# A mixer and mixture-of-experts kernel: a ninth weight slot, a bias write on another queue, and a rebuilt router chain

## The reference

```python
# first block: two layers of three kinds of attention behind one input projection
h = _layernorm(x, ln_in_g, ln_in_b)
for layer in range(2):
    proj = einsum('bsd,de->bse', h, w_in[layer])
    ya, yb, yc = differential(proj), forgetting(proj), stick_breaking(proj)
    y = concat([ya, yb, yc]) @ w_out[layer]
    h = _layernorm(alpha * h + y, ln_g[layer], ln_b[layer])

# second block: sparse attention and a state-space mixer, then 32 experts, 4 per token
mod = silu(c) @ w_ada + b_ada                    # sh_m, sc_m, g_m, sh_f, sc_f, g_f
h = _rms(x, norm_mix) * (1 + sc_m) + sh_m
mixed = sigmoid(g_attn) * y_attn + sigmoid(g_ssd) * y_ssd
x = x + g_m * (mixed @ w_out)
h = _rms(x, norm_ffn) * (1 + sc_f) + sh_f
x = x + g_f * _moe(h, ...)

# _moe
logits = h @ w_router + b_router                 # 256 x 32
top_val, top_idx = top_k(logits, 4)
gates = softmax(top_val)
# each expert, on its tokens: gu = xb @ w_gu[e] + b_gu[e]; clipped SwiGLU;
# out = act @ w_dn[e] + b_dn[e], weighted with the gate and summed per token
```

## Time and profile before

| what | value |
|---|---|
| median of three runs | 1664.46 us (1664.18 to 1669.3) |
| profiled execution | 1668.54 us, span 1666.7 us |
| PE busy | 1564.5 us (94% of the span) |
| DVE, ACT, POOL busy | 417.0, 280.5, 20.1 us |
| chain that ended last | PE 74%, DMA 18%, DVE 4%, ACT 2% |
| mean rate of the DMA engines | 309 GB/s |
| bytes read from HBM | 511.21 MB |

### The profile page before, as it was taken

One profiled execution on the slowest core, in us unless ns is written; L12 is line 12 of the kernel. 1 busy time (PEld: TensorE's weight loads), 2 busy tenths in 40 slices (PEclk: granted clock), 3 DMA queues, 4 the chain that ended last, 5 costly groups with the idle time before them and its releaser, 6 DMA issues.

```text
span 1666.7 us, 18564 instructions
## 1 busy us (share of the span) xinstructions
PE 1564.5 (94%) x7605; PEld 878.2 (53%) x7605; DVE 417.0 (25%) x926; ACT 280.5 (17%) x555; POOL 20.1 (1%) x41
## 2 busy tenths in 40 slices
PE   7989999997999999989999999999999999998997
PEld 6757878685887778853333333333332333333232
DVE  2432113512345381232111211121211112111111
ACT  1224113323232332121000000000000000000000
POOL 4000000000000000000000000000000000000000
PEclk9989999998999999999999999999999999999999
DMA  9765563547232423639999999999999999999996
GB/s 258 194 199 193 185 220 103 200 174 269 101 126 85 152 101 132 266 140 430 423 427 427 427 427 428 428 428 428 427 427 428 428 428 428 427 428 428 427 427 290
DMA packets 83775, 515.17 MB, mean 309 GB/s; under 512 B 4892, under 2 KB 8252, under 8 KB 59144
## 3 DMA queue, kind: packets, MB, share of 16 engines
q1 hardware_dynamic: 82488, 513.45, 76.5%
q0 software_dynamic: 1200, 0.92, 0.7%
q10 hardware_dynamic: 32, 0.01, 0.0%
HBM read 511.21 MB, written 3.15 MB: 309 GB/s over the span
## 4 chain that ended last, share of the span: by engine, by line
PE 74%; DMA 18%; DVE 4%; ACT 2%; issue 1%; SPq 0%; ACTq 0%; DVEq 0%
PE psum L482 25%; PE psum L1109 19%; PE psum L1197 10%; DMA w_down<-in_w_gu 8%; DMA ring<-in_w_gu 8%; PE psum L1083 4%; PE psum L491 3%; DMA ring<-in_w_in 3%; PE psum L1092 2%; PE psum L1100 1%; PE psum L541 1%; PE psum L522 1%; PE psum L627 1%; PE psum L1185 1%; DVE hidden L2137 1%
## 5 line engine op out<-in xcount | busy, mean ns | idle before, releaser
L482 PE MATMUL psum<-spare,ring 128*128 128x256 f32 x1504 | 335.7, 383 | 4.8 <-ACT spare L1421 4.3
L482 PEld LDWEIGHTS psum<-spare,ring 128*128 128x128 f32 x1504 | 285.6, 191 | 54.7 <-issue 15.4
L1109 PE MATMUL psum<-ring,hg 128*64 128x512 f32 x1024 | 229.4, 596 | 8.1 <-DMA ring<-in_w_gu 8.0
L1109 PE MATMUL psum<-w_down,hg 128*64 128x512 f32 x768 | 172.5, 596 | 8.9 <-DMA w_down<-in_w_gu 8.9
L1109 PEld LDWEIGHTS psum<-ring,hg 128*64 128x64 f32 x1024 | 69.8, 137 | 152.0 <-issue 135.2
L1197 PE MATMUL psum<-ring,hiddenT 128*64 128x512 f32 x512 | 113.4, 595 | 13.9 <-ACT hiddenT L1648 10.9
L1109 PEld LDWEIGHTS psum<-w_down,hg 128*64 128x64 f32 x768 | 52.3, 137 | 120.9 <-issue 104.1
L2128 DVE TENSOR_SCALAR gu<-psum 128x512 f32<-128x512 f32 x32 | 22.1, 692 | 329.8 <-PE psum L1109 329.8
L2140 DVE TENSOR_TENSOR o_slot<-psum,gain_rows 128x512 f32<-128x512 f32 x32 | 22.1, 692 | 320.5 <-PE psum L1197 320.5
L1197 PE MATMUL psum<-w_down,hiddenT 128*64 128x512 f32 x384 | 85.9, 595 | 12.9 <-issue 7.7
L1197 PEld LDWEIGHTS psum<-ring,hiddenT 128*64 128x64 f32 x512 | 38.0, 137 | 79.0 <-issue 79.0
(11 more groups left out here) (406 smaller groups left out, 1318.9 us busy)
## 6 DMA issues: line engine op xcount, KB each, us to landing
ring<-in_w_gu SPq DMA_DIRECT2D x64, 2048.0 KB, 27.6
w_down<-in_w_gu SPq DMA_DIRECT2D x48, 2048.0 KB, 28.2
ring<-in_w_dn SPq DMA_DIRECT2D x32, 2048.0 KB, 31.8
ring<-in_w_in SPq DMA_DIRECT2D x24, 2048.0 KB, 9.1
w_down<-in_w_dn SPq DMA_DIRECT2D x24, 2048.0 KB, 31.0
spare<-in_w_gu SPq DMA_DIRECT2D x16, 2048.0 KB, 29.0
ring<-in_w_ada SPq DMA_DIRECT2D x12, 2048.0 KB, 9.2
spare<-in_w_dn SPq DMA_DIRECT2D x8, 2048.0 KB, 33.1
```

Of the source, the lines that this page charges most:

```text
L482: mm = pe.matmul(bank[0:m, c * T:(c + 1) * T], w[:, k, c0 + c * P:c0 + c * P + m], src[:, k, :], start=(i == 0), stop=(i == k_n - 1))
L1109: mm = pe.matmul(psum[half * CAP:(half + 1) * CAP, loop_bank(4 + part), :], hg[:, k, side, :], w[:, c0:c0 + 512], start=False, stop=(k == ...
```

## The change

- **A ninth slot.** `xT`, `condT`, `mod_rows`, `stat`, `biasrev` and `w_router` become parts of one tile `nine` of 16 KB per partition, in the same total size. The experts use it as ninth slot once `xT` has been read for the last time (`residual` at 4). `SLOTS` is 9, an expert's loads go round nine slots, two experts are written out ahead of a loop over six, and SP's conditions follow. The load into `spare` waits for the router's products instead of the last copy of `h_tok`.
- **The bias write** is issued by POOL, after `w_router`'s load, instead of by SP after `ada0`.
- **Norms.** The last norm of the first block squares each pair of chunks on ACT one pair behind its normalisation; "m." then neither loads the table nor squares. Of the eight sums of squares of "f.", four stand ahead of the last output product.
- **Router.** Three residual groups stand ahead of the router, the transposes of all chunks come first, then the eight router products one after the other in the eighth bank; the fourth residual group follows when DVE has read the logits. The choice is made by `max` over 32 logits, a copy of the four largest, `match_replace` of these by -3e38, and one comparison, for both token blocks. Positions and `pick` are made at once, the gates after them; the turned gates come inside the first expert, ahead of its third put. Of the rows of positions, three and the memset come after the gates.

```diff
@@ the slots
-    FOURS = NE // 4
-    SLOTS = 8
+    SIXES = (NE - 2) // 6
+    SLOTS = 9
@@ PE
             for i in range(2):
                 features(f"wo{2 * j + i}", w, zg, 256 * i, 2)
+                if j and not i:
+                    square_sums_of("f.", range(0, 4))
             last_of(f"wo{j}", f"wo{2 * j + 1}")
-        norm_sums("f.", None)
-        take("router4")
+        square_sums_of("f.", range(4, KC))
+        def residual(k):
+            b, j = k // 2, k % 2
+            for i in range(4):
+                mm = pe.matmul(psum[:, loop_bank(k), i * P:(i + 1) * P], xT[:, 4 * j + i, b * P:(b + 1) * P],
+                               ident[:, :], start=(i == 0), stop=False, skip_group_check=True)
+            mm.then_inc(ev("residual"), 1)
+        for k in range(3):
+            take(f"sum{k}")
+            residual(k)
...
-            mm = pe.matmul(psum[q, banks["router4"][0], 0:T], w_router[:, c, :], hT[:, c, :],
-                           start=(c < 4), stop=(c >= 4), skip_group_check=True)
...
+        for c in range(KC):
+            q = slice(32 * (c % 4), 32 * (c % 4) + 32)
+            mm = pe.matmul(psum[q, BANKS, 0:T], w_router[:, c, :], hT[:, c, :], start=(c < 4), stop=(c >= 4),
+                           skip_group_check=True)
+        mm.then_inc(ev("router4"), 1)
...
+        pe.wait_ge(ev("logits_read"), 1)
+        residual(3)
...
-        pe.wait_ge(ev("chosen"), 1)
+        pe.wait_ge(ev("selected"), 1)
         bank = take("pos")
...
+        def turn_gates():
+            for b in range(NB):
+                for half in range(2):
+                    pe.matmul(psum[half * HEAD:half * HEAD + NE, loop_bank(7), T + b * P:T + (b + 1) * P],
+                              rt[:, 1, b, :], ident[:, :], start=True, stop=True)
@@ SP
-            if name == "ada0":
-                read_out(sp, "bias")
-                sp.dma_start(bias_dram[:, :, :], biasrev[:, :].rearrange("h (o j) -> h o j", o=1)
-                             .broadcast_to([AH, P, 2 * T])).then_inc(ev("bias_out"), 16)
...
-            if j < 2:
-                sp.wait_ge(ev(f"down_done{j}"), n - 1)
-            elif j < 5:
-                sp.wait_ge(ev("gu_used"), 3 * n + j - 4)
+            if j == 0:
+                sp.wait_ge(ev("gu_done"), 2 * n - 2)
+            elif j < 3:
+                sp.wait_ge(ev(f"down_done{j - 1}"), n - 1)
             else:
-                sp.wait_ge(ev("gu_done"), 2 * n)
+                sp.wait_ge(ev("gu_used"), 3 * n + j - 5)
...
-        read_out(sp, "ht11")
+        sp.wait_ge(ev("router4"), 1)
         load(0, 1, 1, 1)
-        for j in range(2, 6):
+        sp.wait_ge(ev("residual"), 4)
+        load(0, 1, 1, 2)
+        for j in range(3, 6):
             load_after(0, 1, 1, j)
@@ POOL, after the load of w_router
+        read_out(pool, "bias")
+        pool.dma_start(bias_dram[:, :, :], biasrev[:, :].rearrange("h (o j) -> h o j", o=1)
+                       .broadcast_to([AH, P, 2 * T])).then_inc(ev("bias_out"), 16)
@@ ACT, in norm
+                if then_square and j:
+                    square(n, j - 1)
+            if then_square:
+                square(n, 3)
@@ DVE
         for b in range(NB):
-            top_sum(rt[:, 2, b, :], rt[:, 0, b, :], rt[:, 3, b, :], rt[:, 4, b, :],
-                    rsm[:, 8 * b + TOPE - 1:8 * b + TOPE], rsm[:, 16 + b:17 + b], rsm[:, 18 + b:19 + b], TOPE)
+            ch.after(dve.match_replace(rt[:, 3, b, :], four[:, b, :], rt[:, 2, b, :], -3e38))
+        tt(rt[:, 0, :, :], rt[:, 3, :, :], rt[:, 2, :, :], ALU.is_lt, ev("selected"))
```

More of the change, by code:

```diff
@@ L282, in mixer_moe_kernel @@
     rsm = sb("rsm", [P, 32], where=third)
+    four = sb("four", [P, NB, 8], where=third)
     pos = sb("pos", [P, NB, 5, NE], where=third)
@@ L536, in norm_sums, with square_sums_of @@
                 ada(aside)
-            bank = take(tag + "var")
-            for c in range(KC):
+            square_sums_of(tag, range(KC))
+        def square_sums_of(tag, cs):
+            if cs[0] == 0:
+                take(tag + "var")
+            bank = psum[:, banks[tag + "var"][0], :]
+            for c in cs:
                 if c % 2 == 0:
@@ L1065, in _ @@
         full(mm, "count")
-        bank = take("gateT")
-        for b in range(NB):
-            for half in range(2):
-                mm = pe.matmul(bank[half * HEAD:half * HEAD + NE, b * P:(b + 1) * P], rt[:, 1, b, :], ident[:, :],
-                               start=True, stop=True)
-        full(mm, "gateT")
         M = MAX_EXTRA
@@ L1402, in exp_table, with norm @@
             act.preload_act_table_set("natural_log_exp_and_others")
-        def norm(tag, centred, scale, shift, dst, e):
-            exp_table()
+        def norm(tag, centred, scale, shift, dst, e, squared=False, then_square=False):
             n = norms[0]
             norms[0] += 1
-            for j in range(4):
+            if not squared:
+                exp_table()
+            for j in range(0 if squared else 4):
                 r = slice(2 * j, 2 * j + 2)
@@ L1624, in _ @@
         ins.then_inc(ev("gate_exp"), 1)
-        rows_of_tokens(0, 1)
-        rows_of_tokens(1, 1)
-        for half in range(2):
-            r = slice(half * HEAD, half * HEAD + NE)
-            read("gateT", gateT[r, :], cols=slice(0, T), rows=r, last=half == 1)
         def gathered(n, width=2, first_bank=4):
@@ L1651, in _ @@
         gathered(1, first_bank=6)
+        act.wait_ge(ev("turned"), 1)
+        for half in range(2):
+            r = slice(half * HEAD, half * HEAD + NE)
+            act.activation(gateT[r, :], psum[r, loop_bank(7), T:2 * T], ACT.Copy).then_inc(ev("gateT"), 1)
         expert(0, 0)
@@ L2051, in _ @@
         both = lambda v: v.rearrange("p (b e) -> p b e", b=NB)
-        ch.after(dve.tensor_copy(quarters[:, :], product(dve, "router4")[:, 0:T]), ev("router_parts"))
+        ch.after(dve.memset(four[:, :, :], 3e38))
+        dve.wait_ge(ev("router4"), 1)
+        ch.after(dve.tensor_copy(quarters[:, :], psum[:, BANKS, 0:T]), ev("router_parts"))
         dve.wait_ge(ev("logits"), 1)
-        ch.free(dve.tensor_tensor(rt[:, 2, :, :], both(product(dve, "router4")[:, T:T + NB * NE]),
-                                  over(b_router[:, :], NB), ALU.add), "router4")
+        tt(rt[:, 2, :, :], both(psum[:, BANKS, T:T + NB * NE]), over(b_router[:, :], NB), ALU.add, ev("logits_read"))
@@ L2071, in _ @@
+        tt(rt[:, 0, :, :], rt[:, 3, :, :], rt[:, 2, :, :], ALU.is_lt, ev("selected"))
         ch.free(dve.scalar_tensor_tensor(rt[:, 3, :, :], both(product(dve, "pos")[:, 0:NB * NE]), 1.0, rt[:, 0, :, :],
                                          ALU.add, ALU.mult), "pos")
[L2073 to L2075 removed]
+        ts(pos[:, :, 0, :], rt[:, 3, :, :], -1.0, None, ALU.add)
@@ L2102, in _ @@
         ins.then_inc(ev("picked"), 1)
+        dve.wait_ge(ev("gate_exp"), 1)
+        for b in range(NB):
+            stt(rt[:, 5, b, :], rt[:, 5, b, :], 1.0, rt[:, 0, b, :], ALU.mult, ALU.mult,
+                accum_out=rsm[:, 22 + b:23 + b])
+        ch.after(dve.reciprocal(rsm[:, 24:26], rsm[:, 22:24]))
+        for b in range(NB):
+            ts(rt[:, 1, b, :], rt[:, 5, b, :], rsm[:, 24 + b:25 + b], None, ALU.mult)
         for side in (0, 1):
@@ L2106, in _ @@
         ins.then_inc(ev("gates"), 1)
+        for r in range(1, 4):
+            ts(pos[:, :, r, :], rt[:, 3, :, :], -1.0 - CAP * r, None, ALU.add)
+        ch.after(dve.memset(pos[:, :, 4, :], -1.0))
         ts(passes[:, 1:2], passes[:, 0:1], CAP + 0.5, None, ALU.is_gt)
```

107 lines of the change are left out of this document (45 added, 62 removed).

## The result

The changed kernel takes **1650.06 us** (median of four runs, 1648.38 to 1653.79) against 1664.61 us (1664.18 to 1669.3) for the kernel before on the same chip: ratio 0.991, 95% interval 0.989 to 0.9933. That is 14.6 us faster; 12.3 had been forecast, to 1652. The profiled execution of it took 1648.38 us, its span is 1646.5.

The account below looks back on a forecast made before the run. The end was set by when the weight stream restarts for good plus the loads left; slot -4.9, router chain -6.7, norm -2.7 and bias write +2 sum to -12.3 us, giving 1652, range 1638 to 1661.

Parts of the forecast that it names:

- Ninth slot, -4.9: Expert weight stream: the ninth slot's load is hidden before the restart, leaving 183 loads instead of 184, -4.9 us.
- Rival E: Expert stage: the slot does nothing, as PE sets the pace or the ninth load is late; 1657 us, chance 0.08.
- Sums of squares, +1.1: Norm ahead of the router: four of eight sums moved before the last output product make PE end later, +1.1 us.
- Residual groups in the wait for h, 0: Ahead of the router: three residual groups, 2.9 us, just fit PE's wait for the normalised h, cost 0.
- Router products in strips, with the copy at -2.7: Router: eight products overlap in four 32-column strips, 1.00 us, so the `quarters` copy starts 2.7 us earlier, the +1.1 included.
- VectorE's choice, -3.4: Router's choice of experts: fewer operations, and gates moved behind the picks, cut 5.4 us to 2.0, -3.4 us.
- Three position ops and a memset ... -0.6: Path to the first gather: these ops leave it, -0.9, the experts' bias product ends slightly after the picks, +0.3; -0.6 us.
- Norm of the first block, -2.7: Mixer's first block, last norm: earlier squares and no table load end the sums near 407.0 instead of 409.76, -2.7 us.
- Between 0 (order harmless) and +4.2 I take +2: Bias write moved to POOL's queue: packet-for-packet sharing delays loads in the kernel's start, 0 to +4.2, taken as +2 us.
- rival B: Kernel's start: the bias write gets out of the loads' way, -10 instead of +2, 1640 us, chance 0.20.
- Rival D: Kernel's start: POOL's write goes first on its 8 engines by long packets, +21.3, 1671 us, chance 0.07.
- Rival C: Router chain gives half: strips not overlapping, low clock in the transposes, norm at 0; 1658 us, chance 0.15.

Follow-up runs that it names:

- the second trace: The changed kernel run and profiled once more with nothing edited: 1650.39 us, ratio 0.9909 against the kernel before.
- `b_gu` first: Against the changed kernel, SP issues the load into `spare` only after POOL's four small gate/up bias loads have landed: 1647.86 us, ratio 0.9898.
- three at once: Changed kernel plus bias write from 128 partitions, eight sums of squares together, and `spare` load held until the gate/up bias lands: 1640.73 us, ratio 0.9857.

## Why the prediction was right, step by step

The sign held, and so did the argument on what bounds the kernel: the restart of the stream and the loads behind it. 1650.06 lies in the range and 2 us from the figure, but that it is so near is in part luck. The router chain gave 2.2 to 2.7 us less than forecast, the bias write 5 to 7 us more and by another mechanism than the one forecast, the norm 1.1 us more.

- **What bounds the kernel: right.** The end follows the restart: 15.42 us of the profile's 20.2 came by an earlier restart, 4.84 by one load less.
- **Ninth slot, -4.9: right.** 4.84 in the trace; 4.7 in the trace and 4.25 by medians when undone. Rival E is out.
- **Sums of squares, +1.1: right.** 1.22 measured up to the copy. PE idled 0.96 us ahead of the last of them.
- **Residual groups in the wait for h, 0: right.** Three groups take 2.84 us, and the transposes wait for ACT (0.70, 0.26 and 0.33 us), not ACT for PE.
- **Router products in strips, with the copy at -2.7: right.** 1.07 us for the eight, and the stretch to the copy is 42.97 - 40.60 = 2.4 shorter, the +1.2 in it. The 3.4 us of products that do not overlap did not come. To the restart the placement alone is worth 0.7 to 1.2 us, since without it there is no wait for `b_gu`.
- **VectorE's choice, -3.4: right.** 5.38 became 1.99. A `MATCH_REPLACE8` on 32 elements takes 0.18 us, its value load 0.09; I had bounded the two together by 0.28. The old choice puts the restart only 0.8 to 1.2 us later, for the same reason.
- **"Three position ops and a memset ... -0.6": the step that failed in the chain.** From the copy to the gather I had 5.9 to 6.0 us and measured 7.38 and 7.69. I gave the bias product 0.3 us behind the picks. It waited 0.74 us for `b_gu` (1.41 in the second trace), because the load into `spare`, which the change issues earlier, shares the engines with it; and then it ran 2.08 us at the low clock, where it takes 1.13 at the high. The prediction had hidden two loads "inside the time in which the stream stands still" and asked what they would do to PE's end, not what they would do to a small load that was due in that time. The window from 716 to 726 us shows the new traffic (columns as in the earlier trace rows; in the same ten microseconds counted from the copy, 729.25 to 739.25, the kernel before moved 210 GB/s):

```profile
716.00:726.00 10.00, 8.72 (x48) 6.91 (x48) 5.64 (x33) 1.90 (x4) 0.00 (x0) 0.66 0.96 398
```

  The low clock holds into the gather, 5.28 us instead of 4.84. So the chain from the output products to the restart gained 61.43 - 56.90 = 4.5 us (4.0 in the second trace), not 6.7. With `b_gu` first it gains 61.43 - 55.08 = 6.35 us, nearly the forecast, and 7.4 with the sums together as well (three at once).
- **Norm of the first block, -2.7: right, mis-sized.** 3.8 measured, within the ends of 0 and -4.6. After the table load is gone, the eight sums take 5.25 us in the chain and not 6.16, as only part of them meets the low clock.
- **"Between 0 (order harmless) and +4.2 I take +2": the term that failed.** It was -3 to -5: -3 to -4 by the traces (second value products at 111.0 in the mean instead of 114.1 and 115.3), -4.8 by the median. Both premises of the +2 were half right, and the prediction took the wrong side between them. Packets do go one for one, as I had worked out. But I summed up the engines' time as if the write would give some of it to the loads. It kept its 49 GB/s and the loads' 24 GB/s came on top, as fits a pace set at the source partitions and not by the order on the engines; that it is set there, the write from all partitions shows. It is rival B's mechanism, with about half its price or less: not all of a wait of 6.75 us and the clock behind it is gone, since one load packet per write packet is a slow pace too, and the next two loads were late by 0.92 and 3.37 us. B's full 10 us come when the write itself is fast: by medians 4.8 from the queue and 5.3 from the partitions, by the start of the second value products 115.31 - 106.23 = 9.1 in all.
- **Rival D, slower: out.** The Trainium skill, DMA: Bandwidth & Descriptors, section Queues, rings and completion order, has 9 to 17 descriptors as typical for a packet. That does not hold here: POOL's packets held 4096 bytes, two of the write's rows of 2048 bytes, and in 4 us there were as many load packets as write packets (48 each); the long packets that rival D needs did not occur.
- **Rival C, half the chain: out as priced.** The strips overlapped and the norm gave its gain. Only the low clock came, and elsewhere: at the bias product and the gather, not in the transposes.

The sum by measured pieces is 4.8 (slot) + 4 (write) + 3.8 (norm) + 4.0 to 4.5 (chain), about 17 us, between the 14.6 of the medians and the 20 of the profiles. By medians alone slot, write and norm are 4.3 + 4.8 + 2.3 = 11.4, which leaves 3 for the chain. The two accounts differ by the scatter of executions of 1 to 4 us, in which the low stretches have their part; closer than that these runs do not settle it.

## What to carry to other kernels

When a stream of weights sets the end, price a change by two numbers only: when the stream starts for good, and how many loads lie behind that moment. When an edit fills an idle stretch of the DMA engines, look up which small transfers are due in just that stretch, and let the bulk go behind them. And before a slow transfer is moved to another queue, ask why it is slow: spreading its source over all partitions made it nearly four times as fast and gained about as much again as moving it. And when several steps of a chain get faster at once, ask which arrival they all wait for next: here it was a load of 64 KB that had had 10 us to spare before (its last packet ended at 725.35, the product that reads it began at 735.56).

## What the hardware showed that I had not expected

- A write of 2 MB from 8 partitions holds at 49 to 51 GB/s, alone and beside loads, of which as many packets of 2 KB pass as of its 4 KB packets (48 and 48 in 4 us); from 128 partitions a 4 KB packet takes 159 ns instead of 591, and the write lands in 13.1 us instead of 48.1, with the engines together at up to 421 GB/s.
- A load of 64 KB took 5.3 us to land while one of 2 MB in another queue had begun; the median of the four such loads was 2.2 us.
- The granted clock's low stretches, here of 3.4, 6.8 and once 10.2 us, come at other places in two executions of the same kernel (at 30 us in one, at 100 us in the other), and one on the path cost up to 2.7 us (44.63 against 41.97). A profile's difference of 20 us was 14.6 in the medians.
